# Differential attention, rows 4 to 7: the second bank of transposed weights is copied by ScalarE

## What is computed

```python
    def block(args):
        q_i, i = args                       # 128 query rows, all 8 heads
        ...
        sc = jnp.einsum('bqhtd,bkhtd->bhtqk', q_i.astype(jnp.float32), kf) * scale
        p = jax.nn.softmax(jnp.where(mask, sc, neg), axis=-1)
        w = p[:, :, 0] - lam * p[:, :, 1]
        return jnp.einsum('bhqk,bkhe->bqhe', w, vf)
    ...
    o = rmsnorm(o, sub_norm_b[j]) * (1.0 - lambda_init)
    y = (o * jax.nn.silu(gate)) @ w_out_b[j]
```

## Time and profile before

| | us |
|---|---|
| median of 3 runs | 3305.14 |
| lowest, highest | 3303.95, 3306.03 |
| the profiled execution, its own time | 3299.93 |
| its span | 3298.3 |
| of it, the loop of 7 differential heads | 549.1 (from 2531.5 to 3080.6) |
| the last differential head | 79.4 (3080.6 to 3160.0) |

### The profile page before, as it was taken

The page is one execution under the profiler, slowest core; times in us unless marked ns, Lnnn a source line. Parts: engine busy times, 40 slices in busy tenths (PEclk is TensorE's granted clock), DMA queues, the critical chain, the costliest instruction groups (busy, mean ns, idle before and its releaser), DMA issues.

```text
span 3298.3 us, 35192 instructions
## 1 busy us (share of the span) xinstructions
PE 2831.9 (86%) x13183; PEld 2241.0 (68%) x13198; DVE 1642.0 (50%) x2184; ACT 795.1 (24%) x1269; POOL 110.8 (3%) x124
## 2 busy tenths in 40 slices
PE   5528998797999999996899999999967999999784
PEld 4406666575777777775788888888845777776563
DVE  5672444434545544446444443445454666656533
ACT  3224434212111111113111111011132334333411
POOL 0330000000000000000000000000000000000000
PEclk9759999798999999998999999999988999999887
DMA  5101111032334333331322222222223122212112
GB/s 198 64 0 64 52 51 38 33 121 102 140 127 150 138 129 129 137 138 68 128 77 88 76 76 87 78 76 76 76 81 139 64 65 65 67 64 65 40 51 102
DMA packets 49394, 290.69 MB, mean 88 GB/s; under 512 B 6336, under 2 KB 6464, under 8 KB 19392
## 3 DMA queue, kind: packets, MB, share of 16 engines
q0 software_dynamic: 14544, 105.91, 9.5%
q1 hardware_dynamic: 15872, 110.61, 9.5%
q10 hardware_dynamic: 18928, 73.48, 6.2%
HBM read 248.03 MB, written 33.55 MB: 85 GB/s over the span
## 4 chain that ended last, share of the span: by engine, by line
PE 74%; DVE 15%; ACT 4%; issue 3%; DMA 2%; ACTq 0%; DVEq 0%; SPq 0%
PE PB L226 12%; PE PB L228 12%; PE PB L227 12%; PE OBB L226 7%; PE OBB L228 7%; PE OBB L227 7%; PE OBB L847 5%; PE PB L807 4%; PE TBB L761 4%; DVE cacc L666 2%; PE PB L289 1%; DVE small L1011 1%; DMA xs<-A 1%; DVE V L1345 1%; DVE PT L1035 1%
## 5 line engine op out<-in xcount | busy, mean ns | idle before, releaser
L226 PE MATMUL PB<-HH,WH 128*128 128x512 f32 x1520 | 598.7, 394 | 54.9 <-DVE HL L352 25.5
L227 PE MATMUL PB<-HL,WH 128*128 128x512 f32 x1520 | 596.4, 392 | 0.0
L228 PE MATMUL PB<-HH,WL 128*128 128x512 f32 x1520 | 595.9, 392 | 0.0
L226 PE MATMUL OBB<-HH,WH 128*128 128x512 f32 x992 | 402.8, 406 | 11.7 <-DVE WL L242 11.7
L228 PE MATMUL OBB<-HH,WL 128*128 128x512 f32 x992 | 389.7, 393 | 0.0
L227 PE MATMUL OBB<-HL,WH 128*128 128x512 f32 x992 | 388.7, 392 | 0.0
L226 PEld LDWEIGHTS PB<-HH,WH 128*128 128x128 f32 x1520 | 288.8, 190 | 121.0 <-issue 33.7
L228 PEld LDWEIGHTS PB<-HH,WL 128*128 128x128 f32 x1520 | 288.4, 190 | 60.7
L227 PEld LDWEIGHTS PB<-HL,WH 128*128 128x128 f32 x1520 | 288.9, 190 | 60.0
L242 DVE TENSOR_TENSOR WL<-RAW,WH 128x2048 fp32r<-128x2048 f32 x101 | 230.7, 2285 | 84.2 <-DMA WH<-units 51.9
L953 ACT ACTIVATE E<-PB,small 128x128 f32<-128x128 f32 (+3 forms) x192 | 142.3, 742 | 333.8 <-DVE small L1014 293.2
(11 more groups left out here) (264 smaller groups left out, 3581.6 us busy)
## 6 DMA issues: line engine op xcount, KB each, us to landing
WH<-units POOLq DMA_DIRECT2D x85, 1024.0 KB, 5.0
RAW<-units SPq DMA_DIRECT2D x85, 1024.0 KB, 4.7
gs<-units ACTq DMA_DIRECT2D x16, 1024.0 KB, 4.8
gu<-gs ACTq DMA_DIRECT2D x16, 1024.0 KB, 3.9
RAW<-gu SPq DMA_DIRECT2D x16, 1024.0 KB, 4.8
WH<-gu POOLq DMA_DIRECT2D x16, 1024.0 KB, 5.1
xs<-A ACTq DMA_DIRECT2D x3, 4096.0 KB, 15.2
XR<-xs ACTq DMA_DIRECT2D x2, 4096.0 KB, 12.8
```

What stands on the lines that cost most here:

```text
L226: first = pe.e.matmul(out, wh, xh, start=start, stop=False)
L227: pe.e.matmul(out, wh, xl, start=False, stop=False)
L228: return pe.e.matmul(out, wl, xh, start=False, stop=stop), first
```

## The change

`second_bank(t)` is new in ScalarE's list, behind `halves_out(t)` and ahead of `high_tile` and `exps` of the row. For rows 4 to 7 of every differential head it waits for the transposes of the second bank and copies the bank to `PT0`. VectorE's `out_of_banks` leaves that bank out. `values(t)` waits for both copies, and the next row's transposes into `TB[1]` wait for ScalarE's.

```diff
@@ turn(t)
+                        elif t > 4 and g and not forget:
+                            pe.e.wait_ge(act_done, at_mark(pe, "act", f"pt0_{t - 1}_1", i))
@@ values(t)
-                    pe.e.wait_ge(dve_done, at_mark(pe, "dve", f"pt{c}_{t}_{g}", i))
+                    if g and not forget:
+                        pe.e.wait_ge(act_done, at_mark(pe, "act", f"pt{c}_{t}_1", i))
+                        pe.e.wait_ge(dve_done, at_mark(pe, "dve", f"pt{c}_{t}_0", i))
+                    else:
+                        pe.e.wait_ge(dve_done, at_mark(pe, "dve", f"pt{c}_{t}_{g}", i))
@@ attend_act
+            def second_bank(t):
+                if not forget and t >= 4:
+                    e.wait_ge(pe_done, at_mark(act, "pe", f"T0_{t}_1", i))
+                    e.activation(PT0[:, 4:t + 1, :], TB[1][:, 0:(t - 3) * P].rearrange("p (b n) -> p b n", n=P),
+                                 ACT.Copy).then_inc(act_done, act.mark(f"pt0_{t}_1"))
...
                 halves_out(t)
+                second_bank(t)
@@ out_of_banks(t)
-                    for g in range(1 if t < 4 else 2):
+                    for g in range(1 if t < 4 or not forget else 2):
```

## The result

The changed kernel takes **3320.32 us** (median of 14 executions, 3305.88 to 3326.20), the kernel before 3304.61 (14 executions, 3299.20 to 3306.03). The ratio is 1.0044, with a 95% interval of 1.0030 to 1.0057: slower by 0.44%, or 15.7 us. Its executions spread over 20 us, those of before over 7 in this set and over 9 to 13 in the sets measured later. The profiled one is near the lower end of its own spread, at 3306.01 us.

The account below looks back on a forecast made before the run. TensorE, busy for 86% of the span, was taken to bound the kernel. Seven heads of 1.67 + 0.54 - 0.09, less 0.09, gave +14.7 us on the median 3305.14, so 3320; the forecast's own range was 3312 to 3328.

Parts of the forecast that it names:

- The reason: In rows 4 and 5 the new ScalarE copy stands behind four DMA issues, which hold it until they end.
- Row 4, +1.67 us: In each loop head, values(4) gets a new 1.46 us wait for ScalarE's copy, plus 0.21 for a slower matmul group.
- Row 5, +0.54: In each loop head, values(5) starts 0.54 us later because the issues hold the copy, where 0.33 could have been won.
- Row 6, nothing: No DMA issues here; the copy ends under the scores, so nothing is gained or lost.
- Row 7, -0.09: ScalarE's copy of 512 columns takes 0.60 us in place of VectorE's 0.69, a gain of 0.09 a head.
- The last head: No swaps issued, so row 4's value matmuls do not wait; row 7 gains 0.09 us; head as long as before.
- The sum: Whole kernel: 7 x (1.67 + 0.54 - 0.09) - 0.09 = +14.7 us.
- The clock: Clock falls cost 12.7 us in the loop; half of that gained or lost is 6 us.
- rival B: Clock falls get fewer in the loop, as heads of 78.7 us meet fewer: 5 to 10 us back, chance 0.09.
- two of seven: Count of loop heads with the clock up; a number quite other than this would show the forecast wrong.
- A's: Rival: new waits bring one more clock fall in each head, 10 to 18 us, so 3330 to 3338; chance 0.14.
- Rival C: Issues do not hold the copy; VectorE and ScalarE copy side by side, 3.0 us gained, so 3302; chance 0.05.

Follow-up runs that it names:

- the doubled issues: Changed kernel with eight DMA issues in place of four in rows 4 and 5 of the loop: 3363.57 us against 3303.25 for the kernel before.
- row 4 only: Kernel before with only row 4's second bank copied by ScalarE, rows 5 to 7 left with VectorE: 3324.81 against 3301.67 us, ratio 1.0063.
- the padding: Two kernels: the kernel before with eight or sixteen transposes repeated in each loop head, no new wait: 3318.30 and 3320.50 us against 3303.25.
- the order "ahead": Changed kernel with rows 4 and 5's ScalarE copy ahead of halves_out: 3289.45 against 3301.67 us for the kernel before; again, 3293.77 against 3300.52.

## Why the prediction was right

The forecast was +14.7 us on 3305.14, so 3320, slower than before. Measured: 3320.3, and +15.7 against before's runs of the same set. Step by step:

- **The reason.** The four DMA issues hold ScalarE's next instruction. Right, and shown three ways: by the copy's start 0.11 us after they end, by its recovery when it stands ahead of them, and by the doubled issues. The evidence before the run was two exponentials that moved with the end of the issues.
- **Row 4, +1.67 us.** Measured 1.72. The wait itself was 1.52 where 1.46 was forecast, since TensorE started 0.12 us after ScalarE's copy, not 0.05 as after VectorE's. The longer group after a wait (0.21) was right: ten matmuls in 1.38 against 1.17 in the chain. The copy took the 0.28 us of the sum; the lower bound given for it, 0.30, was above that and so was no bound.
- **Row 5, +0.54.** Measured 0.54. The wait grew by 0.63 (1.02 to 1.65), and 0.08 came back in the next wait for the weights (from 1.73 to about 1.65).
- **Row 6, nothing.** Measured -0.09: the wait for row 7's weights fell from 2.09 to 2.02 or 2.03. This is small and repeats in each head; its cause was not followed.
- **Row 7, -0.09.** Mis-sized: -0.18 (the wait went from 0.94 to 0.76). I read it from the second head, whose clock was down in row 7, so its transposes ended late and VectorE's first copy was already out of the way. With the clock up, the second copy queues behind the first, and ScalarE saves more. A head of before with the clock up, row 7, VectorE's two copies in one piece and TensorE:

```profile
2755.03 1.29 DVE L1035 COPY PT<-TBB 128x512 f32<-128x512 f32 x2 [0.82 <-PE TBB L761]
...
2756.38 2.05 PE L847 MATMUL OBB<-vt,PT 128*128 128x128 f32 x16 [0.94 <-DVE PT L1035]
```

- **The last head.** `values(4)` has no wait, as said, and the wait of `values(7)` went from 0.88 to 0.73. But the head was not as long as before: from its row 4 to the end of the kernel it is 184.0 us before and 182.2 after, with granted clocks of 0.71 and 0.83 in its rows 4 to 7. Other kernels lie between 182.5 and 184.9 there. This was not taken apart further.
- **The sum.** Clean heads went from 76.65 to 78.64, +1.99 where +2.12 was forecast. Seven are 13.9 us.
- **The clock.** Here the forecast was lucky in part. It took the falls as unchanged and put +-6 us on them. In the median execution they cost 2 us more by subtraction (15.7 less 13.9; no trace is of that execution). But single executions lie from 3305.9 to 3326.2, and the profiled one is rival B at work: it lost only 6 us against before's profiled one, and it has at least four clean heads, where the prediction itself named a number quite other than two of seven as a sign of being wrong. The mean granted clock of the executions goes from 0.942 in the quickest to 0.935 in the slowest. B's reason, "heads of this length meet fewer falls", was right for some executions and wrong for others, and so was A's. The experiments with row 4 only (+11 us beyond its sum) and with the padding (+9 and +5) show that an effect of this size could as well have stood on top of the 14. The forecast had no row by which to exclude that.
- **Rival C**, side-by-side copies and a gain: not in this kernel, but the order "ahead" gives what it described, a gain of 0.70 us a head where its sum had 0.42. The rule of the Trainium skill ("PSUM — Partial Sum Buffer", section "Specifications (TRN2)"), that both engines read PSUM at full bandwidth while they keep to different banks, agrees with these traces: ScalarE's copy of 128 columns took 0.28 us behind the issues, alone, and 0.28 in the order "ahead", where VectorE copied the other bank at the same time, and VectorE's copy of 512 columns took 0.69 us either way. What decided was when ScalarE came to it.

## What to carry to other kernels

Before work is moved to an engine that is idle for 76% of the time, look at what stands ahead of it in that engine's own list at that moment: here four DMA issues of 2.44 us together, which the busy share does not count. The same copies lost 2.0 us a head behind them and won 0.7 ahead of them. And where TensorE has waits of 1 to 2 us in a loop, compare the distances between fixed points of a pass with the clock up; the total also carries the falls of the clock, which can change by as much as the forecast or more.

## What the runs showed of the hardware

- Four DMA issues occupied ScalarE for 2.44 us (0.51 the first, 0.61 each of the others) whether each moved 32x512 or 32x128 float32, and for 3.0 to 3.4 in row 3 of the first head. The copy behind them started 0.11 to 0.12 us after the last.
- TensorE started 0.12 to 0.14 us after the end of a ScalarE copy (0.10 in the last head), and 0.05 to 0.06 after a VectorE copy (0.15 in the last head).
- 6.1 us of added matmul work (7 x 0.87) cost 15 us, and 12.3 us cost 17. The traces show the difference as a lower granted clock, 0.94 in place of 0.96 over the loop. Totals of kernels with such waits differ by up to 11 us beyond what their instructions explain.
